# One of five gathered token chunks takes its U products from the dense pass

## The chip, the core and the metric

The program runs on one core of one Trainium2 chip. The metric is the time of one execution on the device in microseconds. TensorE is PE, VectorE is DVE, ScalarE is ACT, GpSimd is POOL, SyncE is SP. TensorE's full clock is 2.4 GHz; a granted clock of 0.50 is 1.2 GHz.

## The reference

One decoder layer on 1024 tokens of 1024 channels: a token mixer with a layer norm, then a PEER expert network with a layer norm. The change touches the expert network alone. For each token it scores 2 x 128 keys for each of 8 heads, picks the best 16 of the key pairs of each head (128 experts of 16,384), and computes

```
act = gelu(x . u_tab[idx])            # 128 dot products of length 1024 per token
out = sum over e of (g[e] * act[e]) * v_tab[idx[e]]
```

where g is the softmax over a head's 16 sums. `u_tab` and `v_tab` are 16,384 x 1024 in float32, 64 MB each.

## The kernel before

The tokens are eight chunks of 128. Chunks 0 to 4 are computed **sparse**: for each of the 128 experts of a chunk, GpSimd gathers one row per token (128 rows of 4 KB, 0.52 MB) into a ring of five slots (`gather_rows`), and DVE either reduces it against the tokens (`L143`, rows of U, into `hid`) or adds it with its factor (`L149`, rows of V, into `acc`). A chunk has 256 such steps, first 128 of U, then 128 of V; steps are numbered from 0 to `NROW` - 1 = 1279 over all five chunks and are called **rows** here. Chunk c has rows 256c to 256c + 255. A gather waits until the row five places back is used. Rows 0 to 448 lie beside earlier stages (projection, attention, merge, scores); `R_SCORE` is 449.

Chunks 5 to 7 are computed **dense** in `ffn`. The U pass (`table_block`) goes over all 16,384 experts in 128 blocks: a block of U is loaded into a ring of four (issued from ACT), PE makes 8 matmuls of 384 columns (3 chunks of 128 tokens), ACT applies gelu (`L1794`) and stores the result to `h` in DRAM. In three windows of 16 blocks (from blocks 30, 58 and 86), the weight matrix of one dense chunk is made from one-hot tiles: DVE makes them (`onehots`, `L1831`), ACT scales them (`gated`, `L1765` and `L1766`), PE multiplies them (`weight_group`, `L1697` and `L1698`, 32 groups a window), ACT copies them out, and the SP queue stores 8 MB. The V pass goes over the 128 blocks again: for each four blocks DVE multiplies the reloaded weights and h (`product`, `L1839`), and PE makes 6 matmuls a block with V (`L1716`).

**What sets the order.** Every engine runs its own list in the order of the code. DVE's list is a list of rows: `dense_row(u)` names the row that goes with block u, one-hots, products and the pieces of `choose` (136 steps that pick the experts of one chunk) stand ahead of fixed rows, so DVE's progress in rows and PE's progress in blocks bind each other at the one-hots and at the products. Before, 2.3 rows go with each block of either pass: the U pass is rows 455 to 749, the V pass rows 749 to 1044, the last product (31) stands ahead of row 1037, and 236 rows come after the V pass. `CHOICE_SPAN` places the choices of chunks 5, 6, 7, 3 and 4. After the last row DVE makes the layer norm of chunk 4 and of the three dense chunks.

Of the kernel before, what the change touches and what calls it, by code (L numbers as in the profile page):

```python
# [7 lines left out]
ALU = mybir.AluOpType  # L8
ACT = mybir.ActivationFunctionType
# [6 lines left out]
P = 128  # L16
D = 1024
# [24 lines left out]
NR = 5  # L42
NROW = 2 * NSEL * NSP
NT = 136
# [60 lines left out]


def gather_rows(nc, pool, M, A, a, b):

    ring = M["ring"]
    for n in range(a, min(b, NROW)):  # L110
        c, r = divmod(n, 2 * NSEL)
# [17 lines left out]
def use_rows(nc, dve, M, a, b):  # L129

    ring, hid, gg, acc, used = M["ring"], M["hid"], M["gg"], M["acc"], M["used"]
    for n in range(a, b):
        c, r = divmod(n, 2 * NSEL)
        e = r % NSEL
        x1 = M["x1"](c)
        if r == NSEL:
            dve.wait_ge(M["hid_gelu"], c + 1)
            nc.vector.tensor_tensor(hid[:, c % 2, :], hid[:, c % 2, :], gg[:, c, :], ALU.mult)
            dve.drain()
# [1185 lines left out]
def choose(nc, dve, M, S, sco, c, o, k0, k1):  # L1325
# [9 lines left out]
    for k in range(k0, k1):  # L1335
# [97 lines left out]
        elif k == 133:  # L1433
            ka, kb = keys_of[:, 0, :], keys_of[:, 1, :]
            if c < NSP:
                nc.vector.scalar_tensor_tensor(idx[:, c, :], ka, float(NKEY), kb, ALU.mult, ALU.add)
            else:
                if c - NSP >= 2:
                    dve.wait_ge(S["tri_mm"], c - NSP - 1)
                nc.vector.tensor_copy(pick[:, (c - NSP) % 2, 0:2, :], keys_of)  # L1440
# [96 lines left out]
for _j in range(NBLK // 4):  # L1537
    PRODUCT_AT.setdefault(min(dense_row(NBLK - 2 + 4 * _j), NROW - 1), []).append(_j)
GELU_BLOCK = {2: int((2 * 2 * NSEL + NSEL - R_SCORE - 6) / ROWS_A_BLOCK)}
EXP_BLOCK = {5: 21, 6: 48, 7: 76, 3: 108}  # L1540


def ffn(nc, ctx, M, A, out):
# [102 lines left out]
    @block.gpsimd  # L1646
    def _(pool):
        def finished(c, k):
            pool.wait_ge(sparse_done, k)
            pool.dma_start(out[P * c:P * c + P, :], x1(c)).then_inc(sparse_stored, 16)  # L1650

        for n in range(R_MERGE + NR, NROW):
            gather_rows(nc, pool, M, A, n, n + 1)
            if n == 600:
                finished(0, 1)
                finished(1, 2)
            if n == 3 * 2 * NSEL + 40:
                finished(2, 3)
            if n == 4 * 2 * NSEL + 40:
                finished(3, 4)  # L1660
        finished(4, 5)

    @block.tensor
    def _(pe):
        turn_row(pe, M, XROWS[0], 0, turned)
        for i in range(NX):
# [3 lines left out]
            score_row(pe, M, i, s_out, s_mm, True)  # L1670
        pe.wait_ge(x1t_done, ND)
        pe.wait_ge(s_out, 4 * NX)

        def table_block(u):
# [46 lines left out]
    def _(act):  # L1721
        def high(i):
            act.wait_ge(turned, i + 1)
            if i >= 2:
                act.wait_ge(s_mm, 4 * (i - 2) + 4)
            d = XROWS[i] - NSP
            if d >= 0:
                act.activation(x1t[:, :, P * d:P * d + P],
# [48 lines left out]
        for u in range(NBLK):  # L1777
# [14 lines left out]
            if u % 4 == 0 and g4 >= 2:  # L1792
                act.wait_ge(h_st[g4 % 2], 16 * (g4 // 2))
            act.activation(hout[g4 % 2][:, u % 4, :], ps[:, 4 + u % 4, 0:DT], ACT.Gelu).then_inc(h_out, 1)  # L1794
            if u + 4 < NBLK:
                act.dma_start(ut[u % 4], A["u_t"][u + 4]).then_inc(u_in[u % 4], 16)
            if u % 4 == 3:
                act.wait_ge(h_out, u + 1)
                act.dma_start(A["h"][g4], hout[g4 % 2]).then_inc(h_st[g4 % 2], 16)
# [6 lines left out]
        gate_exps(act, M, S, CHOICES.index(4))  # L1806
        for c in (3, 4):
            gate_hidden(act, M, c)

    @block.vector  # L1810
    def _(dve):
# [34 lines left out]
        for i in range(NX):  # L1846
            low(i)
            if i == 2:
                dve.wait_ge(iota_in, 16)
            if i >= 2:  # L1850
                pick_chunk(2, 34 * (i - 2), 34 * (i - 2) + 34)
            use_rows(nc, dve, M, *SCORE_ROWS[i])
        for n in range(R_SCORE, NROW):
# [172 lines left out]
def build_mix(nc, ctx, A, out):  # L2026
# [61 lines left out]
    with ExitStack() as late:  # L2088
# [100 lines left out]
```

## Time and profile before

| | us |
|---|---|
| median of 3 runs | 3952.82 (3951.11 to 3956.78) |
| profiled execution, its own time | 3949.0 |
| its span, first to last instruction | 3947.2 |
| busy PE / DVE / ACT / POOL | 2912.5 / 2829.9 / 810.7 / 1646.3 |

The profile is one execution. A share of busy time over the whole span mixes stages with different limits, so the rows of the last section are cut by stage. A POOL instruction is the making of one gather's descriptors, not its transfer. PE's matmul durations overlap each other; the spacing of what follows them is the safer measure.

### The profile page before, as it was taken

To read this page: it belongs to the slowest core of one execution; us is meant where nothing else is said; L and a number is where in the kernel's file an instruction comes from. 1 tells how busy PE (TensorE), PEld (TensorE's weight loads), DVE (VectorE), ACT (ScalarE), POOL (GpSimd) and SP (SyncE) were. 2 spreads that over 40 slices of the span, in tenths; PEclk is the share of its full clock that TensorE was granted. 3 is DMA by queue.
4 is the path that set the end of the run, shared out by engine and by line. 5 is a ranking of instruction groups with operands and counts; after the bars stand their busy time and mean duration, and the time that the engine had idled before them with its cause. 6 is when DMAs were issued, how large, how long until landed. Compare 5 with 4: busy or idle time off the path is not lost.

```text
span 3947.2 us, 40352 instructions
## 1 busy us (share of the span) xinstructions
PE 2912.5 (74%) x14133; PEld 1731.2 (44%) x14161; DVE 2829.9 (72%) x5410; ACT 810.7 (21%) x1885; POOL 1646.3 (42%) x1321
## 2 busy tenths in 40 slices
PE   7479819965999986763996889899798999960000
PEld 5458406553666553421453545465343444420000
DVE  5646485966777566966878969794777666677777
ACT  6334101112222221100110829281000000000000
POOL 5200002233444334744344333342544545667774
PEclk9779959987999898986998999899899999985555
DMA  9369224445878558977698898999999999999996
GB/s 293 117 244 391 91 79 161 154 150 184 268 259 265 186 200 333 369 251 289 218 369 305 266 371 301 382 315 375 359 385 383 390 408 408 407 332 321 315 321 216
DMA packets 309467, 1127.62 MB, mean 286 GB/s; under 512 B 33425, under 2 KB 43281, under 8 KB 305937
## 3 DMA queue, kind: packets, MB, share of 16 engines
q0 software_dynamic: 185040, 673.79, 47.6%
q1 hardware_dynamic: 101184, 358.97, 24.2%
q10 hardware_dynamic: 23040, 92.28, 6.4%
q8 instruction: 113, 1.85, 0.2%
q14 instruction: 90, 0.73, 0.1%
HBM read 996.46 MB, written 128.45 MB: 285 GB/s over the span
## 4 chain that ended last, share of the span: by engine, by line
DMA 22%; DVE 16%; POOL 8%; PE 3%; issue 3%; DVEq 1%; ACT 0%; ACTq 0%
DMA rows<-v,expert_ids 14%; DMA rows<-u,expert_ids 8%; POOL rows L117 8%; DVE rows L143 4%; DVE row_sums L149 4%; DVE branches L1831 3%; PE ps L102 1%; PE ps L104 1%; PE ps L103 1%; PE ps L1679 1%; DVE scores_in L1424 0%; DVE shared_64k L1839 0%; DVE best_key_ids L1355 0%; DVE key_sums L1429 0%; DVE scores_in L1347 0%
## 5 line engine op out<-in xcount | busy, mean ns | idle before, releaser
L117 POOL DMA_INDIRECT rows<-u,expert_ids x640 | 796.2, 1244 | 1335.1 <-DVE hidden_sums L143 821.2
L117 POOL DMA_INDIRECT rows<-v,expert_ids x640 | 770.4, 1204 | 796.9 <-DVE row_sums L149 649.9
L149 DVE SCALAR_TENSOR_TENSOR row_sums<-rows,hidden_sums,row_sums 128x1024 f32<-128x1024 f32 x630 | 796.8, 1282 | 319.3 <-DMA rows<-v,expert_ids 316.3
L1679 PE MATMUL ps<-turned_rows,mixer_state 128*128 128x384 f32 x2048 | 686.1, 495 | 23.0 <-DMA mixer_state<-u_t 22.2
L1716 PE MATMUL ps<-shared_64k 128*128 128x512 f32 x1536 | 669.6, 598 | 43.4 <-DVE shared_64k L1839 43.4
L143 DVE CUSTOM_DVE_ANT_0 rows<-rows,branches 128x1024 f32<-128x1024 f32 x384 | 468.4, 1222 | 174.4 <-DMA rows<-u,expert_ids 169.5
L1679 PEld LDWEIGHTS ps<-turned_rows,mixer_state 128*128 128x128 f32 x2048 | 391.9, 194 | 288.8 <-DMA mixer_state<-u_t 24.1
L1716 PEld LDWEIGHTS ps<-shared_64k 128*128 128x128 f32 x1536 | 294.1, 192 | 418.7 <-issue 418.6
L102 PE MATMUL ps<-x_hi_t_b,shared_64k 128*128 128x384 f16 x912 | 300.6, 330 | 89.5 <-DMA shared_64k<-w_pairs_kept 88.6
L143 DVE CUSTOM_DVE_ANT_0 rows<-rows,x_first 128x1024 f32<-128x1024 f32 x256 | 305.2, 1224 | 43.4 <-DMA rows<-u,expert_ids 40.8
L103 PE MATMUL ps<-x_lo_t_b,shared_64k 128*128 128x384 f16 x912 | 300.3, 329 | 0.0
L104 PE MATMUL ps<-x_hi_t_b,shared_64k 128*128 128x384 f16 x912 | 299.9, 329 | 0.0
L1765 ACT ACTIVATE branches<-branches,picks_t 128x128 f16<-128x128 f16 x384 | 151.2, 394 | 77.2 <-DVE branches L1831 76.7
L126 ACT ACTIVATE hidden_sums<-hidden_sums 128x128 f32<-128x128 f32 x5 | 1.5, 309 | 801.6 <-DVE hidden_sums L143 801.6
L102 PEld LDWEIGHTS ps<-x_hi_t_b,shared_64k 128*128 128x128 f16 x912 | 90.5, 99 | 148.7 <-DMA shared_64k<-w_pairs_kept 89.1
L1766 ACT ACTIVATE branches<-branches,picks_t 128x128 f16<-128x128 f16 x384 | 150.6, 392 | 0.0
L1794 ACT ACTIVATE branches<-ps 128x384 f32<-128x384 f32 x128 | 62.3, 487 | 384.8 <-PE ps L1679 384.7
L1831 DVE TENSOR_TENSOR branches<-picks_t,iota_sb 128x512 f16<-128x512 f32 x192 | 123.0, 683 | 0.8
L104 PEld LDWEIGHTS ps<-x_hi_t_b,shared_64k 128*128 128x128 f16 x912 | 90.1, 99 | 60.6 <-issue 2.7
L103 PEld LDWEIGHTS ps<-x_lo_t_b,shared_64k 128*128 128x128 f16 x912 | 90.1, 99 | 56.3 <-issue 2.4
L460 DVE SCALAR_TENSOR_TENSOR shared_64k<-conv_in_b,dw_sb_b,shared_64k 128x768 f32<-128x768 f32 x120 | 113.1, 1027 | 0.0
L1697 PE MATMUL ps<-branches 128*128 128x128 f16 x384 | 53.8, 227 | 76.7 <-ACT branches L1766 76.7
(530 smaller groups left out, 4609.6 us busy)
## 6 DMA issues: line engine op xcount, KB each, us to landing
mixer_state<-u_t ACTq DMA_DIRECT2D x128, 512.0 KB, 7.4
shared_64k<-v SPq DMA_DIRECT2D x128, 512.0 KB, 7.7
rows<-strips SPq DMA_DIRECT2D x32, 768.0 KB, 6.7
h_kept<-branches ACTq DMA_DIRECT2D x32, 768.0 KB, 9.9
shared_64k<-weights_kept SPq DMA_DIRECT2D x32, 768.0 KB, 10.9
shared_64k<-h_kept SPq DMA_DIRECT2D x32, 768.0 KB, 14.6
shared_64k<-s_pairs_kept SPq DMA_DIRECT2D x32, 512.0 KB, 6.7
rows<-w_t SPq DMA_DIRECT2D x30, 512.0 KB, 5.6
```

The costliest lines, as they stand in the source:

```text
L102: pe.matmul(out, a_hi, b_hi, start=first, stop=False)
L103: pe.matmul(out, a_hi, b_lo, start=False, stop=False)
L104: return pe.matmul(out, a_lo, b_hi, start=False, stop=last)
L117: nc.gpsimd.indirect_dma_start(ring[:, n % NR, :], None, A["u" if r < NSEL else "v"], bass.IndirectOffsetOnAxis(ap=M["idx"][:, c, e:e + 1] ...
L143: nc.vector.tensor_tensor_reduce(src, src, x1, 1.0, 0.0, ALU.mult, ALU.add, hid[:, c % 2, e:e + 1]).then_inc(used, 1)
L149: nc.vector.scalar_tensor_tensor(acc[:, e % 2, :], src, hid[:, c % 2, e:e + 1], acc[:, e % 2, :], ALU.mult, ALU.add).then_inc(used, 1)
L460: nc.vector.scalar_tensor_tensor(acc, src, w, acc, ALU.mult, ALU.add).then_inc(tap, 1)
L1679: m = pe.matmul(ps[:, 4 + u % 4, 0:DT], uk[u % 4][:, k, :], x1t[:, k, :], start=k == 0, stop=k == KD - 1)
L1716: m = pe.matmul(ps[:, 2 + 2 * d + half, :], pr[j // 4 % 3][:, d, j % 4, :], vt[j % 6][:, 512 * half:512 * half + 512], start=j == 0, stop= ...
L1765: act.activation(ah[:, n % 4, t, :], o1[:, n % 4, t, :], ACT.Copy, scale=pt[:, 3, tok])
L1766: ins = act.activation(o1[:, n % 4, t, :], o1[:, n % 4, t, :], ACT.Copy, scale=pt[:, 2, tok])
L1831: ins = nc.vector.tensor_tensor(to[:, n % 4, :, :], pt[:, f, 4 * q:4 * q + 4].rearrange("p (t o) -> p t o", o=1).to_broadcast([P, 4, NKEY] ...
```

## The change

Chunk 4 (`HYB`) becomes a hybrid. Its tokens are a fourth group of 128 columns in the U pass: each of the 8 matmuls of a block has 512 columns (`UT`) for 384. ACT makes a second gelu from columns 384 to 511 into a small tile and, for each pair of blocks, stores it to a new DRAM array `h_side` (16,384 x 128 tokens, 8.4 MB, runs of 512 bytes). The 128 gathers of U rows for chunk 4 are gone, `NROW` is 1152. In their place GpSimd makes 128 gathers of one number per token from `h_side` straight into `hid` (`gather_values`), one ahead of each row gather from row 878 (`VALUES_FROM`) on. DVE waits for all of them at row 1024, where the V rows of chunk 4 begin.

The pace is changed too: 2.9 rows go with a block of the U pass and 2.1 with a block of the V pass. The U pass is rows 453 to 824, the V pass rows 824 to 1093, the last product stands ahead of row 1080, and 59 rows come after the V pass. The choices of chunks 5, 6, 7, 3 are spread over rows 453 to 511, 522 to 589, 603 to 670 and 690 to 757, that of chunk 4 over rows 777 to 870 (before: 451 to 497, 509 to 561, 573 to 627, 637 to 701, 737 to 837). The gelu of chunk 2 moves on ACT from block 80 to block 64.

```diff
+HYB = NSP - 1
+UT = DT + P
-NROW = 2 * NSEL * NSP
+NROW = 2 * NSEL * NSP - NSEL
+def row_at(n):
+    c = min(n // (2 * NSEL), HYB)
+    return c, n - 2 * NSEL * c + NSEL * (c == HYB)
...
         if r == NSEL:
-            dve.wait_ge(M["hid_gelu"], c + 1)
+            if c == HYB:
+                dve.wait_ge(M["values_in"], 16 * NSEL)
+            else:
+                dve.wait_ge(M["hid_gelu"], c + 1)
...
-            if c < NSP:
+            if c == HYB:
+                nc.vector.scalar_tensor_tensor(posf[:, 0, :], ka, float(NKEY), kb, ALU.mult, ALU.add)
+                dve.drain()
+                nc.vector.tensor_copy(idx[:, c, :], posf[:, 0, :])
+                nc.vector.tensor_scalar(M["place"], posf[:, 0, :], float(P), M["lane"], ALU.mult, ALU.add)
+            elif c < NSP:
...
-ROWS_A_BLOCK = 2.3
-CHOICE_SPAN = {5: (2, 48), 6: (60, 112), 7: (124, 178), 3: (188, 252), 4: (288, 388)}
+ROWS_U_BLOCK = 2.9
+ROWS_V_BLOCK = 2.1
+CHOICE_SPAN = {5: (0, 20), 6: (24, 47), 7: (52, 75), 3: (82, 105), 4: (112, 150)}
-    return int(R_SCORE + 6 + ROWS_A_BLOCK * u)
+    return int(R_SCORE + 4 + ROWS_U_BLOCK * min(u, NBLK) + ROWS_V_BLOCK * max(u - NBLK, 0))
...
+VALUES_FROM = dense_row(CHOICE_SPAN[HYB][1]) + NR + 3
...
+        def gather_values(e):
+            if e == 0:
+                pool.wait_ge(M["chosen"], HYB + 1)
+                for i in range(2):
+                    pool.wait_ge(side_st[i], 16 * (NBLK // 4))
+            if e < NSEL:
+                nc.gpsimd.indirect_dma_start(
+                    M["hid"][:, HYB % 2, e:e + 1], None, A["h_side"],
+                    bass.IndirectOffsetOnAxis(ap=M["place"][:, e:e + 1], axis=0)).then_inc(M["values_in"], 16)
         for n in range(R_MERGE + NR, NROW):
+            if n >= VALUES_FROM:
+                gather_values(n - VALUES_FROM)
             gather_rows(nc, pool, M, A, n, n + 1)
...
-                m = pe.matmul(ps[:, 4 + u % 4, 0:DT], uk[u % 4][:, k, :], x1t[:, k, :], start=k == 0, stop=k == KD - 1)
+                m = pe.matmul(ps[:, 4 + u % 4, 0:UT], uk[u % 4][:, k, :], x1t[:, k, :], start=k == 0, stop=k == KD - 1)
...
-            act.activation(hout[g4 % 2][:, u % 4, :], ps[:, 4 + u % 4, 0:DT], ACT.Gelu).then_inc(h_out, 1)
+            act.activation(hout[g4 % 2][:, u % 4, :], ps[:, 4 + u % 4, 0:DT], ACT.Gelu)
+            if u % 2 == 0 and u >= 4:
+                act.wait_ge(side_st[u // 2 % 2], 16 * (u // 4))
+            act.activation(side[:, u // 2 % 2, u % 2, :], ps[:, 4 + u % 4, DT:UT], ACT.Gelu).then_inc(h_out, 1)
...
+            if u % 2:
+                act.wait_ge(h_out, u + 1)
+                act.dma_start(A["h_side_blocks"][u // 2], side[:, u // 2 % 2]).then_inc(side_st[u // 2 % 2], 16)
```

## Rows read from the trace of the kernel before

**Rows 1.** The page, the span in 40 equal slices, busy tenths.
```profile
PE   7479819965999986763996889899798999960000
PEclk9779959987999898986998999899899999985555
```

**Rows 2.** Busy time by stage: us, PE, PEld, DVE, ACT, POOL; PEclk, DMA.
```profile
1978.00:2184.00 206.00, 164.50 (x524) 97.18 (x524) 174.73 (x444) 32.16 (x75) 92.38 (x84) 0.89 0.90 335
2184.00:2378.00 194.00, 165.89 (x690) 101.31 (x688) 162.26 (x433) 105.34 (x314) 65.08 (x63) 0.92 0.90 324
2378.00:2563.00 185.00, 166.06 (x709) 101.40 (x708) 158.64 (x407) 108.16 (x326) 68.76 (x66) 0.94 0.93 348
2563.00:2667.00 104.00, 102.26 (x510) 63.99 (x509) 97.69 (x227) 90.86 (x281) 41.07 (x38) 1.00 0.90 314
2667.00:2806.00 139.00, 130.39 (x399) 76.14 (x397) 71.24 (x90) 14.76 (x28) 42.92 (x40) 0.98 0.98 378
2806.00:2829.00 23.00, 0.00 (x1) 0.00 (x0) 18.53 (x24) 1.77 (x2) 14.40 (x13) 0.55 0.97 353
2829.00:3518.00 689.00, 668.61 (x1534) 293.95 (x1535) 482.20 (x742) 1.90 (x3) 378.98 (x301) 0.98 1.00 387
3518.00:3698.00 180.00, 1.04 (x3) 0.19 (x1) 130.78 (x213) 0.00 (x0) 131.29 (x108) 0.51 0.92 323
3701.00:3913.00 212.00, 0.00 (x0) 0.00 (x0) 163.65 (x131) 0.00 (x0) 156.56 (x125) 0.50 0.89 312
3913.00:3947.00 34.00, 0.00 (x0) 0.00 (x0) 27.16 (x64) 0.00 (x0) 0.57 (x1) 0.50 0.15 62
```

**Rows 3.** Timeline of ACT: start, us, instruction, [idle before <-releaser].
```profile
1998.73 0.49 ACT L1794 ACTIVATE branches<-ps 128x384 f32<-128x384 f32 x1 [4.67 <-PE ps L1679]
2003.89 0.49 ACT L1794 ACTIVATE branches<-ps 128x384 f32<-128x384 f32 x1 [4.67 <-PE ps L1679]
...
2400.84 0.49 ACT L1794 ACTIVATE branches<-ps 128x384 f32<-128x384 f32 x1
...
2432.35 0.49 ACT L1794 ACTIVATE branches<-ps 128x384 f32<-128x384 f32 x1
```

**Rows 4.** Timeline of PE, the first weight product of windows 0 and 1.
```profile
2172.93 0.29 PE L1697 MATMUL ps<-branches 128*128 128x128 f16 x1 [39.74 <-ACT branches L1766]
...
2371.86 0.29 PE L1697 MATMUL ps<-branches 128*128 128x128 f16 x1 [9.81 <-ACT branches L1766]
```

**Rows 5.** Groups in 2829:3518: busy us, mean ns | idle before <-releasers.
```profile
L1716 PE MATMUL ps<-shared_64k 128*128 128x512 f32 x1534 | 668.8, 598 | 43.4 <-DVE shared_64k L1839 43.4
...
L117 POOL DMA_INDIRECT rows<-v,expert_ids x148 | 194.9, 1317 | 139.9 <-DVE row_sums L149 115.1 <-issue 16.6 <-DVE hidden_sums L143 6.6
L149 DVE SCALAR_TENSOR_TENSOR row_sums<-rows,hidden_sums,row_sums 128x1024 f32<-128x1024 f32 x150 | 191.9, 1283 | 113.4 <-DMA rows<-v,expert_ids 113.2
```

**Rows 6.** Timeline of POOL and DVE in 3345:3375.
```profile
3343.72 1.75 DVE L1839 TENSOR_TENSOR shared_64k<-shared_64k 128x1536 f32<-128x1536 f32 x1
3344.07 2.21 POOL L117 DMA_INDIRECT rows<-v,expert_ids  x1 [1.73 <-DVE row_sums L149]
...
3353.52 1.28 DVE L149 SCALAR_TENSOR_TENSOR row_sums<-rows,hidden_sums,row_sums 128x1024 f32<-128x1024 f32 x1 [0.87 <-DMA rows<-v,expert_ids]
...
3353.77 1.85 POOL L117 DMA_INDIRECT rows<-v,expert_ids  x1 [0.30 <-issue]
...
3360.06 0.94 POOL L117 DMA_INDIRECT rows<-v,expert_ids  x1 [0.30 <-issue]
```

**Rows 7.** DMA totals of 1978:2806 and of 2829:3518.
```profile
DMA packets 67801, 281.48 MB, mean 340 GB/s; under 512 B 7438, under 2 KB 7438, under 8 KB 66472
...
DMA packets 76417, 266.64 MB, mean 387 GB/s; under 512 B 7663, under 2 KB 7663, under 8 KB 76394
```

**Rows 8.** Timeline of DVE: the last product, and the end of chunk 4.
```profile
3494.61 1.75 DVE L1839 TENSOR_TENSOR shared_64k<-shared_64k 128x1536 f32<-128x1536 f32 x1
...
3911.68 1.23 DVE L153 TENSOR_TENSOR row_sums<-row_sums 128x1024 f32<-128x1024 f32 x1
```

More of the change, by code:

```diff
@@ L110, in gather_rows @@
     for n in range(a, min(b, NROW)):
-        c, r = divmod(n, 2 * NSEL)
+        c, r = row_at(n)
         e = r % NSEL
@@ L132, in use_rows @@
     for n in range(a, b):
-        c, r = divmod(n, 2 * NSEL)
+        c, r = row_at(n)
         e = r % NSEL
@@ L1517, with block_at @@
 WINDOW_AT = [30, 58, 86]
-ROWS_A_BLOCK = 2.3
-CHOICE_SPAN = {5: (2, 48), 6: (60, 112), 7: (124, 178), 3: (188, 252), 4: (288, 388)}
+ROWS_U_BLOCK = 2.9
+ROWS_V_BLOCK = 2.1
+CHOICE_SPAN = {5: (0, 20), 6: (24, 47), 7: (52, 75), 3: (82, 105), 4: (112, 150)}
 NORM_AT = {520: 0, 528: 1}
 def dense_row(u):
-    return int(R_SCORE + 6 + ROWS_A_BLOCK * u)
+    return int(R_SCORE + 4 + ROWS_U_BLOCK * min(u, NBLK) + ROWS_V_BLOCK * max(u - NBLK, 0))
+def block_at(row):
+    return next(u for u in range(2 * NBLK) if dense_row(u) >= row)
 CHOICE_AT = {}
-for _c, (_a, _b) in CHOICE_SPAN.items():
+for _c, (_u, _v) in CHOICE_SPAN.items():
+    _a, _b = dense_row(_u), dense_row(_v)
     for _n in range(_a, _b):
-        CHOICE_AT.setdefault(R_SCORE + _n, []).append((_c, NT * (_n - _a) // (_b - _a), NT * (_n - _a + 1) // (_b - _a)))
+        CHOICE_AT.setdefault(_n, []).append((_c, NT * (_n - _a) // (_b - _a), NT * (_n - _a + 1) // (_b - _a)))
 ONEHOT_AT = {}
@@ L1538 @@
     PRODUCT_AT.setdefault(min(dense_row(NBLK - 2 + 4 * _j), NROW - 1), []).append(_j)
-GELU_BLOCK = {2: int((2 * 2 * NSEL + NSEL - R_SCORE - 6) / ROWS_A_BLOCK)}
-EXP_BLOCK = {5: 21, 6: 48, 7: 76, 3: 108}
+GELU_BLOCK = {2: block_at(5 * NSEL) - 1}
+EXP_BLOCK = {5: 21, 6: 48, 7: 76, 3: 106}
+VALUES_FROM = dense_row(CHOICE_SPAN[HYB][1]) + NR + 3
 def ffn(nc, ctx, M, A, out):
@@ L1557, in ffn @@
     again = ut
+    side = M["side"]
     iota, pick, pt, gh16 = M["iota"], M["pick"], M["pick_t"], M["gh16"]
@@ L1568, in ffn @@
     h_st = [sem(f"h_stored{i}") for i in range(2)]
+    side_st = [sem(f"side_stored{i}") for i in range(2)]
+    lane_in = sem("lane_in")
     tri_mm, tri_hi, tri_out, tri_lo = (sem(n) for n in "tri_mm tri_hi tri_out tri_lo".split())
@@ L1585, in _ @@
         sp.dma_start(iota[:], A["iota"]).then_inc(iota_in, 16)
+        sp.dma_start(M["lane"], A["iota"][0:1, :].rearrange("o n -> n o")).then_inc(lane_in, 16)
         for d in range(ND):
@@ L1670, in _ @@
             score_row(pe, M, i, s_out, s_mm, True)
-        pe.wait_ge(x1t_done, ND)
+        pe.wait_ge(x1t_done, ND + 1)
         pe.wait_ge(s_out, 4 * NX)
@@ L1725, in high @@
                 act.wait_ge(s_mm, 4 * (i - 2) + 4)
-            d = XROWS[i] - NSP
-            if d >= 0:
+            d = XROWS[i] - NSP if XROWS[i] >= NSP else ND
+            if XROWS[i] >= HYB:
                 act.activation(x1t[:, :, P * d:P * d + P],
@@ L1793, in _ @@
                 act.wait_ge(h_st[g4 % 2], 16 * (g4 // 2))
-            act.activation(hout[g4 % 2][:, u % 4, :], ps[:, 4 + u % 4, 0:DT], ACT.Gelu).then_inc(h_out, 1)
+            act.activation(hout[g4 % 2][:, u % 4, :], ps[:, 4 + u % 4, 0:DT], ACT.Gelu)
+            if u % 2 == 0 and u >= 4:
+                act.wait_ge(side_st[u // 2 % 2], 16 * (u // 4))
+            act.activation(side[:, u // 2 % 2, u % 2, :], ps[:, 4 + u % 4, DT:UT], ACT.Gelu).then_inc(h_out, 1)
             if u + 4 < NBLK:
                 act.dma_start(ut[u % 4], A["u_t"][u + 4]).then_inc(u_in[u % 4], 16)
+            if u % 2:
+                act.wait_ge(h_out, u + 1)
+                act.dma_start(A["h_side_blocks"][u // 2], side[:, u // 2 % 2]).then_inc(side_st[u // 2 % 2], 16)
             if u % 4 == 3:
-                act.wait_ge(h_out, u + 1)
                 act.dma_start(A["h"][g4], hout[g4 % 2]).then_inc(h_st[g4 % 2], 16)
@@ L1806, in _ @@
         gate_exps(act, M, S, CHOICES.index(4))
-        for c in (3, 4):
-            gate_hidden(act, M, c)
+        gate_hidden(act, M, 3)
     @block.vector
@@ L1849, in _ @@
                 dve.wait_ge(iota_in, 16)
+                dve.wait_ge(lane_in, 16)
             if i >= 2:
@@ L1862, in _ @@
                 second_norm(NORM_AT[n])
-            if n >= 2 * 2 * NSEL and n % (2 * NSEL) == 2 * NSEL - 1:
-                second_norm(n // (2 * NSEL))
+            if n >= 2 * 2 * NSEL and row_at(n)[1] == 2 * NSEL - 1:
+                second_norm(row_at(n)[0])
         for d in range(ND):
@@ L2043, in build_mix @@
     M["stage_sems"] = {}
+    M["values_in"] = sem("values_in")
     M["mp_in"] = [sem(f"folded_in{i}") for i in range(4)]
@@ L2063, in build_mix @@
     for n, shape, dt in (("weights", (ND, P, NBLK * P), F32), ("h", (NBLK // 4, P, 4, DT), F32),
+                         ("h_side", (NEXP * P, 1), F32),
                          ("scores", (T // P, P, 2 * H * NKEY), F32), ("x1", (ND, P, D), F32),
@@ L2067, in build_mix @@
         A[n] = nc.dram_tensor(n + "_kept", shape, dt, kind="Internal").ap()
+    A["h_side_blocks"] = A["h_side"].rearrange("(b j e t) o -> b e j (t o)", j=2, e=P, t=P)
     A["v_blocks"] = A["v"].rearrange("(b e) c -> b e c", e=P)
@@ L2097, in build_mix @@
             nc.release_semaphore(handle)
-        M["x1t"] = sb("turned_rows", [P, KD, DT], F32)[:]
+        M["x1t"] = sb("turned_rows", [P, KD, UT], F32)[:]
+        M["place"], M["lane"] = sb("value_places", [P, NSEL], U32)[:], sb("lane_sb", [P, 1], F32)[:]
+        M["side"] = mixa[:, 4 * D:4 * D + 4 * P].rearrange("p (s j t) -> p s j t", s=2, j=2)
         M["sco"] = [sb("scores_in", [P, 2 * H * NKEY], F32)[:]]
```

## The prediction

> **What bounds the kernel now.** The first view is the page's 40 slices: PE is nearly full up to about 3520 us and does nothing after it, at a clock of 0.5 [rows 1]. The second is the busy time by stage [rows 2], where the program splits into four parts.
>
> The U pass runs from 1978 to 2806 (828 us). The timeline of ACT gives PE's pace there: outside the windows one gelu each 5.16 us, with ACT idle before it until PE is done [rows 3]. That is PE's own time: a block is 8 matmuls of 384 columns. Inside window 1 five blocks take 31.51 us, 6.30 each [rows 3]; the extra 1.14 us a block is the weight products. So PE's own time for the pass is 128 x 5.16 + 48 x 1.14 = 715 us, and the other 113 us are stalls. The largest is PE's wait of 39.7 us at the first weight product, a second is 9.8 us [rows 4]: ACT had no one-hots, since DVE had not reached their row. In the stages that hold the windows DVE is busy 0.84 to 0.94 of the time; behind them the DMA share is up to 0.98 [rows 2]. The pass is thus bound by PE, and in places by DVE and the rows that it waits for.
>
> From 2806 to 2829 PE stands still: DVE is late at the row of product 0 [rows 2].
>
> The V pass takes 689 us (2829 to 3518), PE is busy 668.8 of them [rows 5], so 660 = 128 x 5.16 us is its floor (6 x 512 columns are as many as 8 x 384). DMA is at a share of 1.00 and 387 GB/s, DVE waits 113.4 us for rows of V [rows 2, 5]: PE and DMA are both full.
>
> Then come the rows that have no partner: 212 us for 126 rows, 1.68 us each [rows 2]. From the last product at 3494.6 to the end of chunk 4 at 3911.7 there are 417 us and 243 rows [rows 8], and 35.5 us of norms and store up to 3947.2. The end of the kernel is therefore V pass, then leftover rows, then a fixed tail.
>
> **What the change removes.** 128 rows of U (67 MB) go, and the new pace packs more of the rest beside the dense passes: behind the last product stand 1152 - 1080 = 72 rows instead of 243. At 1.68 us that is 121 us, for the 417 of before.
>
> **What it adds to the U pass.** 512 columns for 384: 5.16 x 4/3 = 6.88 us a block, + 1.72 us, 220 us in all. Nothing hides it where PE is the limit; it hides where PE waited. PE's floor becomes 128 x 6.88 + 48 x 1.14 = 935 us. The stalls must be worked out anew.
>
> At the entry, PE reaches block 30 at 1978 + 30 x 6.88 = 2184. DVE reached row 521 and its one-hots shortly before 2173 [rows 4]; now it has to be at row 537, 16 rows x 1.3 us = 21 us further, but the choice of chunk 6 stands mostly behind that row now (about 10 us less). It comes to about 2184, and slower loads of U leave DMA room for rows. I take 5 us of stall for the 40.
>
> For a window, DVE's stage 2563:2667 shows 97.7 of 104 us busy [rows 2], so DVE was full. It gets 0.6 rows x 1.28 us = 0.8 us more a block, 6.4 to 7.2, where PE goes from 6.30 to 8.02. So PE, not DVE, is the limit inside a window. Between windows 12 blocks now take 83 us. Their transfers are 12 x 0.52 MB of U, 12 x 0.20 of h, 12 x 0.07 of `h_side`, 35 rows x 0.52, 8.4 MB of weights and 1 MB of scores, 37 MB; at the V pass's 387 GB/s [rows 7] 96 us. Some of that spills into the windows, where DMA has room. I take 10 us of stall for each of the two gaps, 10 behind window 2 for the same store, 0 at best and 25 each at worst. Sum: 935 + 5 + 30 = 970 us, + 142 on before. Over the whole pass DMA isn't the limit: 281 MB of before [rows 7], 40 MB of rows and 8.4 MB more are 330 MB, 340 GB/s, below the 387 of the V pass. DVE gets 77 rows x 1.28 = 99 us and about half a choice (22 us) more, in 142 us.
>
> The second gelu on ACT (128 columns, about 0.3 us), the wait for its store and one more DMA issue each two blocks add some 0.6 us a block; ACT idles 4.67 us a block outside the windows [rows 3] and is busy 90.86 of 104 in one [rows 2], 5.6 us of a block that grows to 8.0. They cost nothing. What is queued behind ACT's wait for the side store is that block's gelu and the next window's `gated`; the store has two blocks' time, 13.8 us. The gelu of chunk 2 now stands inside window 1 and can hold ACT until row 640; DVE is at row 638 there, so 0 to 5 us, in the stall above. Product 0 stands ahead of row 818, and DVE is no longer late by a store: 4 us for the 23.
>
> **What it adds to the V pass.** A value gather is new; no row shows one. On POOL, a row gather that meets no DVE instruction takes 0.94 us, with 0.30 behind it. One that starts under a DVE instruction ends 0.82 us after that instruction: 3353.77 + 1.85 = 3355.62, where `L149` ended at 3354.80; 3344.07 + 2.21 = 3346.28 against `L1839`'s 3345.47 [rows 6]. The mean of the pass is 1.32 us for rows of V [rows 5]. A value gather also makes one descriptor for each of 128 tokens, so I price it like a row gather: 1.24 us at least, 1.62 at the mean. Row n's gather stands behind value gather n - 878, so POOL spends 2.5 to 3.2 us a row, while PE's pace asks for 5.16 / 2.1 = 2.46. With both engines free about half of the time I take 1.5 us each, 3.0 a row: POOL is the limit for 128 rows, DVE falls behind, the products with it, and PE waits. Cost (3.0 - 2.46) x 128 = 69 us, taken as 65; from 5 to 95.
>
> The Trainium skill (SBUF — State Buffer, "Who interferes with whom") says that an operation with two SBUF inputs takes only the read side of the port that VectorE shares with GpSimd, and infers that making descriptors needs the write side, so that such an operation shouldn't hold a gather up. By it each gather would take 1.24 us, the pair 2.48, and this term would be near nothing. The rows show otherwise [rows 6]: `L1839` and `L149` both have two SBUF inputs and both held a gather.
>
> Transfers: 2.1 rows and one block of V, weights and h are 2.02 MB per 5.16 us, 391 GB/s, what the pass has now (387). The 4-byte packets of the value gathers are not in any row as reads; between nothing and a row packet's time they cost 0 to 163 us (128 x 8 packets an engine x 0.159 us, that being 4096 B at the 412 GB/s / 16 of a full stage). In the 65 us by which POOL stretches the stage there is room for the small end, and I take the small end, as packets under 512 B already are a tenth of all packets [rows 7] beside a full DMA. The Trainium skill (DMA: Bandwidth & Descriptors, "Measured") gives some 10.5 ns as the least for a packet; by that estimate it would be 11 us of DMA time.
>
> Early in the pass PE lost 20 us (43.4 less the 23 at its start [rows 5]) to DVE, busy with chunk 4's choice; half of that choice is done before now: 15 us. V pass: 660 + 15 + 65 = 740 us.
>
> **Sum.** 1978 + 970 + 4 + 740 = 3692 for the end of the V pass. The last product starts 24 us before it, as now (3518 - 3494.6): 3668. Then 1.75 of product [rows 8], 121 of rows, 35.5 of tail: a span of 3826. The profiled execution took 3949.0 for a span of 3947.2, so 3828, or 121 less; off the median 3952.8 that is 3832 us.
>
> **The rivals.** (1) *The value gathers ride free*: POOL's slack, 139.9 us before 148 rows of V [rows 5], 0.95 a row, nearly covers one of 1.24. Against it, the gathers held under DVE. 3832 - 65 = 3767. (2) *The U pass keeps its stalls*: DVE and DMA bind at the windows as now, 113 us instead of 35, since more rows go with each block. For it, DMA shares of 0.90 to 0.98 [rows 2]; against, 33% more PE time a block under only 26% more rows. 3832 + 78 = 3910. (3) *A value gather is much dearer than a row gather*, on POOL in rows 878 to 1005: each microsecond costs 128 us there. It decides from 121 / 128 = 0.95 us above my 1.5, 2.45 us each; at 3 us the kernel takes 3832 + 192 = 4024, slower than before. For it, one gather of 2.21 us [rows 6]; against, that this was a wait for a DVE operation. (4) *Nothing is removed*, which the new `NROW` excludes.
>
> **Chances.** The forecast 0.5, (1) 0.2, (2) 0.2, (3) 0.1, of which 0.07 beyond its point. The range of 3758 to 3902 takes in (1) with a few us less of stalls, and most of (2); what is left out is the far side of (2) and (3). A change of 0.2% (8 us) is about what can be told from none. Faster 0.91, within it 0.02, slower 0.07.
>
> **What would show it.** Gelus of `L1794` 6.88 us apart outside windows; no 40 us wait at the first weight product; a U pass near 970 us. In rows 878 to 1005 POOL without idle time, row steps of 3.0 us, PE waiting for `L1839`; before and behind that, 2.46. After the last product 72 rows at 1.68. The forecast falls if the U pass is over 1010 us, or if PE never waits in the V pass, or if DVE waits at row 1024 for values.

## The result and the profile after

The changed kernel took 3827.66 us (median of 4 runs, 3819.65 to 3836.34) beside 3951.97 before: a ratio of 0.9685, 95% interval 0.9659 to 0.9711. 3832 us was forecast. The profiled execution took 3836.3 us, its span is 3834.5.

| part of the span, us | before | forecast | after |
|---|---|---|---|
| start of the U pass | 1978 | 1978 | 1985 |
| U pass | 828 | 970 | 983 |
| gap before the V pass | 23 | 4 | 2 |
| V pass | 690 | 740 | 739 |
| last product to the end of chunk 4's last row | 417 | 123 | 122 |
| tail | 35.5 | 35.5 | 35.5 |
| span | 3947 | 3826 | 3834.5 |

The last product starts before the V pass ends (24 us before, 32 us after), so the rows add up to more than the span.

The page's slices, for [rows 1]: PE is full to nearly the end, and the stretch at clock 0.5 is gone.

```profile
PE   6579828965999995873799899899999998699960
PEclk9779969977999997996899999999999999799985
```

The stages, for [rows 2], same columns (us, PE, PEld, DVE, ACT, POOL, clock, DMA share, GB/s). The first five are the U pass. The next five are the V pass without its last 31 us, which lie in the eleventh, beside the rows behind the last product. Rows 878 to 1005, those with a value gather ahead of each, are 3115 to 3498.

```profile
1985.00:2214.00 229.00, 211.25 (x503) 94.27 (x504) 193.83 (x472) 34.19 (x95) 104.38 (x99) 0.96 0.93 343
2214.00:2440.00 226.00, 213.08 (x710) 101.08 (x709) 180.44 (x466) 114.28 (x354) 89.19 (x84) 0.97 0.92 333
2440.00:2660.00 220.00, 212.10 (x712) 100.62 (x711) 179.85 (x381) 114.75 (x355) 89.66 (x82) 0.98 0.92 338
2660.00:2785.00 125.00, 125.00 (x500) 61.92 (x499) 113.95 (x271) 93.81 (x294) 54.38 (x48) 1.00 0.91 316
2785.00:2969.00 184.00, 176.94 (x408) 77.75 (x406) 121.03 (x258) 20.02 (x55) 80.36 (x68) 0.98 0.97 372
2969.00:3115.00 146.00, 136.93 (x315) 60.46 (x316) 113.81 (x272) 2.88 (x3) 80.45 (x61) 0.98 0.97 371
3115.00:3242.00 127.00, 121.35 (x277) 52.66 (x276) 66.21 (x72) 0.31 (x1) 100.10 (x89) 0.99 0.93 334
3242.00:3318.00 76.00, 36.20 (x39) 10.59 (x38) 32.59 (x25) 0.00 (x0) 56.32 (x54) 0.54 0.72 230
3318.00:3498.00 180.00, 179.90 (x417) 79.57 (x417) 87.69 (x67) 0.00 (x0) 128.76 (x112) 0.99 0.94 347
3498.00:3678.00 180.00, 180.00 (x421) 79.65 (x420) 117.55 (x103) 0.00 (x0) 95.34 (x77) 1.00 1.01 396
3678.00:3799.00 121.00, 30.59 (x72) 13.26 (x70) 92.01 (x73) 0.00 (x0) 80.56 (x68) 0.64 0.89 321
3800.00:3834.00 34.00, 0.00 (x0) 0.00 (x0) 27.42 (x65) 0.00 (x0) 0.57 (x1) 0.50 0.15 62
```

In the U pass PE is busy 0.92 to 1.00 of each stage. POOL rises to 0.71 to 0.79 busy in the value rows; DMA falls there from 371 GB/s to 334 and 347, and rises to 396 behind them. The stretch 3242:3318 is another matter: PE busy 36 of 76 us at a clock of 0.54. It comes back below.

The gelus of ACT are 6.87 us apart outside windows, 5.16 before [rows 3]:

```profile
2102.40 0.49 ACT L1834 ACTIVATE branches<-ps 128x384 f32<-128x384 f32 x1 [6.21 <-PE ps L1719]
...
2109.27 0.49 ACT L1834 ACTIVATE branches<-ps 128x384 f32<-128x384 f32 x1 [6.21 <-PE ps L1719]
```

PE in that stretch (timeline of the changed kernel). Ahead of each matmul stand up to 1.8 us for which the profile has no releaser; the longest such wait is 3.2 us:

```profile
3257.06 1.87 PE L1756 MATMUL ps<-shared_64k 128*128 128x512 f32 x2 [1.79 <-issue]
3259.89 1.01 PE L1756 MATMUL ps<-shared_64k 128*128 128x512 f32 x1 [0.97 <-issue]
...
3267.67 0.59 PE L1756 MATMUL ps<-shared_64k 128*128 128x512 f32 x1 [1.41 <-issue]
3269.77 1.01 PE L1756 MATMUL ps<-shared_64k 128*128 128x512 f32 x1 [1.51 <-issue]
```

### The profile page after: what moved, and what is told of

Same layout as the page of the kernel before. It is cut to its first block, busy times and chain, and to the rows that moved or that the text cites. A ratio compares the mean times of both kernels' runs of the same rounds, so it can differ in the third digit from the quotient of the medians.

```text
span 3834.5 us, 40292 instructions
## 1 busy us (share of the span) xinstructions
PE 3138.2 (82%) x14133; PEld 1729.4 (45%) x14161; DVE 2667.6 (70%) x5156; ACT 835.9 (22%) x2013; POOL 1613.7 (42%) x1321
## 4 chain that ended last, share of the span: by engine, by line
PE 17%; DMA 14%; POOL 7%; DVE 6%; issue 4%; another core or an unknown queue 3%; ACT 1%; DVEq 0%; SPq 0%; ACTq 0%
PE ps L1719 13%; DMA rows<-v,expert_ids 7%; POOL rows L125 5%; DMA rows<-u,expert_ids 5%; POOL hidden_sums L1686 2%; DVE rows L154 2%; DMA h_side_kept<-mixer_state 1%; DVE row_sums L160 1%; PE ps L104 1%; PE ps L106 1%; PE ps L105 1%; DMA mixer_state<-u_t 1%; PE ps L1737 1%; PE ps L1738 1%
## 5 line engine op out<-in xcount | busy, mean ns | idle before, releaser
L125 POOL DMA_INDIRECT rows<-u,expert_ids x512 | 648.4, 1266 | 1214.0 <-DVE hidden_sums L154 697.1
L125 POOL DMA_INDIRECT rows<-v,expert_ids x640 | 744.8, 1164 | 798.9 <-DVE row_sums L160 632.4
L160 DVE SCALAR_TENSOR_TENSOR row_sums<-rows,hidden_sums,row_sums 128x1024 f32<-128x1024 f32 x630 | 796.0, 1282 | 354.7 <-DMA rows<-v,expert_ids 323.3
L1719 PE MATMUL ps<-turned_rows,mixer_state 128*128 128x512 f32 x2048 | 899.1, 598 | 11.4 <-DMA mixer_state<-u_t 10.7
L1756 PE MATMUL ps<-shared_64k 128*128 128x512 f32 x1536 | 685.0, 605 | 55.7 <-issue 42.9
L154 DVE CUSTOM_DVE_ANT_0 rows<-rows,branches 128x1024 f32<-128x1024 f32 x256 | 310.8, 1219 | 109.3 <-DMA rows<-u,expert_ids 100.6
L1805 ACT ACTIVATE branches<-branches,picks_t 128x128 f16<-128x128 f16 x384 | 153.2, 399 | 43.0 <-DVE branches L1875 42.9
L1686 POOL DMA_INDIRECT hidden_sums<-h_side_kept,value_places x128 | 141.3, 1104 | 39.0 <-issue 39.0
L104 PE MATMUL ps<-branches,shared_64k 128*128 128x384 f16 x192 | 65.6, 342 | 54.8 <-DMA shared_64k<-s_pairs_kept 54.7
```

The source lines that it names most:

```text
L104: pe.matmul(out, a_hi, b_hi, start=first, stop=False)
L125: nc.gpsimd.indirect_dma_start(ring[:, n % NR, :], None, A["u" if r < NSEL else "v"], bass.IndirectOffsetOnAxis(ap=M["idx"][:, c, e:e + 1] ...
L154: nc.vector.tensor_tensor_reduce(src, src, x1, 1.0, 0.0, ALU.mult, ALU.add, hid[:, c % 2, e:e + 1]).then_inc(used, 1)
L160: nc.vector.scalar_tensor_tensor(acc[:, e % 2, :], src, hid[:, c % 2, e:e + 1], acc[:, e % 2, :], ALU.mult, ALU.add).then_inc(used, 1)
L1686: nc.gpsimd.indirect_dma_start(M["hid"][:, HYB % 2, e:e + 1], None, A["h_side"], bass.IndirectOffsetOnAxis(ap=M["place"][:, e:e + 1], axis ...
L1719: m = pe.matmul(ps[:, 4 + u % 4, 0:UT], uk[u % 4][:, k, :], x1t[:, k, :], start=k == 0, stop=k == KD - 1)
```

## Experiments

**The changed kernel again**, twice, nothing edited.

> The changed kernel once more, nothing edited. The first profile has a stretch of some 75 us in the V pass (3242 to 3318) in which PE, DVE and SP all go slowly and the trace names no releaser. If it comes again at the same block, it belongs to the program; if not, to that execution. Expected 3828 us (3815 to 3840) either way, since rows 878 to 1005 still cost POOL 2.8 us each: the stall is then found as PE waits for products, spread over the pass.

> The changed kernel a third time, beside the next two. In three of the four kernels with value gathers ahead of every row one stretch of 50 to 95 us in those rows was slow on all engines with no releaser in the trace; in one (the same program as here) it did not come. If it comes, the time is near 3825 us and the stretch lies in rows 878 to 1005; if not, near 3805.

Measured 3805.6 us, ratio 0.9633 (0.9604 to 0.9662), and 3806.61, ratio 0.9642 (0.9615 to 0.9669). The slow stretch is in neither profile, and both are 21 us faster than the first result. The first expectation, 3815 to 3840 us with or without the stretch, is missed; the second holds. (It counts four kernels with a value gather ahead of every row and leaves out the one with 3.2 rows a block, which had no such stretch either.) The U pass takes 983 us and 978, the V pass 718 and 713. Without the stretch, PE waits for products over the whole of the value rows (groups in the V pass, of the first of the two):

```profile
L1756 PE MATMUL ps<-shared_64k 128*128 128x512 f32 x1536 | 678.2, 604 | 41.0 <-DVE shared_64k L1883 41.0
```

So part of the first result's V pass was that stretch. Comparisons below are with these two repeats.

**The value gathers.**

```diff
-                dve.wait_ge(M["values_in"], 16 * NSEL)
+                pass
...
-            if n >= VALUES_FROM:
-                gather_values(n - VALUES_FROM)
```

> The 128 value gathers and DVE's wait for them are left out (the factors of chunk 4 are then stale numbers); all else stays. Theory, POOL's issue rate sets the pace of rows 878 to 1005 (2.84 us a row against 2.46): the V pass shortens by 45 to 75 us, 3755 to 3783 us in all. Rival, PE and DMA bind the pass anyway: within 15 us of the changed kernel, 3813 to 3828.

Measured 3744.62 us, ratio 0.9475 (0.9451 to 0.9499), 61 us below the kernel beside it; the total expected was reckoned from the first result and is missed, the 45 to 75 us are met. PE's V pass takes 662 us where it took 718: 56 us. POOL's groups in 3107:3475, first with the value gathers, then without:

```profile
L1686 POOL DMA_INDIRECT hidden_sums<-h_side_kept,value_places x124 | 144.3, 1164 | 37.8 <-issue 37.8
L125 POOL DMA_INDIRECT rows<-v,expert_ids x115 | 130.5, 1135 | 36.0 <-issue 34.8 <-DVE row_sums L160 1.2
```

```profile
L125 POOL DMA_INDIRECT rows<-v,expert_ids x144 | 180.2, 1251 | 159.1 <-DVE row_sums L160 129.5 <-issue 13.5 <-DVE row_sums L157 11.0
```

With them POOL has nothing but the 0.30 us behind each instruction as idle time: 37.8 us for 124. It is full, at 1.16 + 0.30 us for a value gather and 1.14 + 0.30 for a row: 2.9 us a row (DVE is at row 880 at 3107.8 us and at row 1000 at 3458.4: 2.92), where PE's pace is 2.46. Without them it waits for used rows. The DMA totals of 3107:3475, with and without:

```profile
DMA packets 39714, 123.74 MB, mean 336 GB/s; under 512 B 7473, under 2 KB 7473, under 8 KB 39704
```

```profile
DMA packets 42454, 147.38 MB, mean 400 GB/s; under 512 B 4198, under 2 KB 4198, under 8 KB 42443
```

With value gathers DMA moves less (336 against 400 GB/s) and has 3275 packets under 512 B more. The trace has their sizes. Every gather, of a row or of values, ends in 16 packets of 4 bytes, and a value gather has 16 packets of 32 bytes beside them (1985 such packets in this stretch for 124 value gathers, none without them), not 128 of 4 bytes. They take 14 ns each. DMA is not what binds there.

**The same gathers, spread.**

```diff
-CHOICE_SPAN = {5: (0, 20), 6: (24, 47), 7: (52, 75), 3: (82, 105), 4: (112, 150)}
+CHOICE_SPAN = {5: (0, 20), 6: (24, 47), 7: (52, 75), 3: (82, 105), 4: (110, 128)}
...
-                gather_values(n - VALUES_FROM)
+                k = n - VALUES_FROM
+                for e in range(2 * k // 3, 2 * (k + 1) // 3):
+                    gather_values(e)
```

> The same 128 value gathers, but two for every three rows over rows 832 to 1023 instead of one a row over 878 to 1005; chunk 4's choice over blocks 110 to 128 so that the places are known in time. Theory, POOL's issue rate is what makes the value gathers cost 56 us in the V pass: three row gathers and two value gathers take 3 x 1.5 + 2 x 1.4 = 7.3 us against 3 x 2.46 = 7.4 of PE's pace, so nearly all of it goes, 3755 to 3785 us. Rival, the packets and the landing of the values cost DMA time: the same number of them costs the same wherever they stand, 3795 to 3815. Second rival: the denser choice costs in the U pass what is won.

Measured 3783.95 us, ratio 0.9557 (0.9533 to 0.9581). The V pass takes 688 us for 718. The number of gathers and of their bytes is the same, so the 30 us go with where they stand on POOL. This run was made on another chip (10) than the repeats (14); the spread kernel further down, on chip 14, has a V pass of 669 us beside a repeat's 713. Of the rest, 12.6 us are one wait of PE for product 1. The expectation of the kernel with the earlier choice, below, lays it to exponentials that ACT makes after the U pass. The trace says otherwise: ACT has them 21 us before DVE uses them, and DVE has no idle time before that. It works without a pause on the last, large steps of the choice, which stand between products 0 and 1:

```profile
2973.41 0.31 ACT L1474 ACTIVATE exponents<-exponents 128x128 f32<-128x128 f32 x1
...
2987.56 2.77 DVE L1435 TENSOR_TENSOR scores_in<-scores_in,key_sums 128x256 f32<-128x256 f32 x8
2990.41 2.29 DVE L1440 TENSOR_REDUCE key_sums<-scores_in 128x128 f32<-128x2048 f32 x1
...
2994.70 0.27 DVE L1458 TENSOR_REDUCE gate_sum<-exponents 128x8 f32<-128x128 f32 x1
```

**Columns alone**, in the kernel before.

```diff
-                m = pe.matmul(ps[:, 4 + u % 4, 0:DT], uk[u % 4][:, k, :], x1t[:, k, :], start=k == 0, stop=k == KD - 1)
+                m = pe.matmul(ps[:, 4 + u % 4, 0:UT], uk[u % 4][:, k, :], x1t[:, k, :], start=k == 0, stop=k == KD - 1)
```

> The kernel before with 512 columns instead of 384 in the matmuls of the U pass, the extra columns used by nobody; rows, pace and gathers as before. Theory, PE's own time binds the U pass and the stalls of DVE shrink as it slows: the pass goes from 828 to 940 to 975 us, 3952 + 110 to 145 = 4062 to 4097 in all. Rival, DVE and DMA bind the pass enough to hide half of the added PE time: under 4030. Second rival, the stalls stay whole: 4172.

Measured 4023.09 us, ratio 1.0177 (1.0149 to 1.0206): 71 us more, below the 110 that my theory gave at least, and within the first rival's bound. Of 220 us of added PE time, 120 were hidden in the U pass and the gap behind it (from the start of one pass to that of the other it is 851 us before, 136 over PE's floor of 715, and 950 here, 15 over the floor of 935), and 25 more in the V pass (690 before, 665 here), since DVE now enters it on time. The sum 220 - 120 - 25 = 75 is near the 71 measured. The pass itself, at 950, lies where I had put it; what I had left out was that the old gap of 23 us and the V pass's stalls go with the U pass's. PE's wait at the weight products, 76.7 us before, of which 39.7 at once [rows 4], is now (waits in the U pass: total, times, longest):

```profile
PE ps L1699 <- ACT branches L1768: 13.6, 5, 10.2
```

**Rows in the U pass, more and fewer.** More: 3.2 a block.

```diff
-ROWS_U_BLOCK = 2.9
-CHOICE_SPAN = {5: (0, 20), 6: (24, 47), 7: (52, 75), 3: (82, 105), 4: (112, 150)}
-EXP_BLOCK = {5: 21, 6: 48, 7: 76, 3: 106}
+ROWS_U_BLOCK = 3.2
+CHOICE_SPAN = {5: (0, 20), 6: (24, 47), 7: (52, 75), 3: (80, 96), 4: (110, 140)}
+EXP_BLOCK = {5: 21, 6: 48, 7: 76, 3: 95}
```

> The changed kernel with 3.2 rows a block in the U pass instead of 2.9; chunk 3's choice over blocks 80 to 96 and chunk 4's over 110 to 140, so that they are in time. 38 rows move from behind the last product into the U pass. Theory, PE binds the U pass and has room for them: 38 x 1.68 = 64 us less behind the V pass, 10 to 40 more in the U pass, 3775 to 3805 us. Rival, the rows of the U pass are at the limit of DVE and DMA: each added row costs there what it saves behind, 3825 us or more.

Measured 3802.2 us, ratio 0.9614 (0.9586 to 0.9643): no change against 3805.6, the intervals overlapping. The time lies in the theory's range only because that was reckoned from 3828; as a difference it is the rival's, no gain. Behind the last product 57 us went (120 to 63), but the U pass and its gap took 1047 us for 983. The two passes, first with 3.2 rows, then with 2.9:

```profile
1974.00:3020.00 1046.00, 947.23 (x2825) 438.45 (x2824) 841.46 (x1968) 378.63 (x1149) 484.12 (x417) 0.95 0.92 340
3020.00:3747.00 727.00, 680.65 (x1536) 297.18 (x1536) 443.18 (x474) 1.90 (x3) 491.66 (x413) 0.97 0.96 358
```

```profile
1977.00:2960.00 983.00, 935.46 (x2825) 434.12 (x2825) 789.17 (x1844) 375.72 (x1148) 436.89 (x379) 0.98 0.93 342
2960.00:3679.00 719.00, 678.22 (x1536) 296.64 (x1536) 445.09 (x558) 3.25 (x5) 486.40 (x412) 0.97 0.96 361
```

DVE gains 52 us of work and the pass 63. But 29 of the 63 lie in blocks 94 to 102, which take 90 us for 61, and into these the edit had pressed chunk 3's choice. So the run doesn't show that the added rows alone cost what they save; 3.2 rows with a choice spread as before were not run.

Fewer: 2.3 in both passes.

```diff
-ROWS_U_BLOCK = 2.9
-ROWS_V_BLOCK = 2.1
+ROWS_U_BLOCK = 2.3
+ROWS_V_BLOCK = 2.3
```

> The changed kernel with 2.3 rows a block in both passes, as before the change; the choices keep their blocks. The last product stands ahead of row 1034, so 118 rows come behind it instead of 72, 77 us more at 1.66. Theory, the U pass then comes near its floor (950 us for 983), and the V pass is bound by POOL in the value rows as now: 3840 to 3870 us. Rival, the pace is worth nothing, since each row costs the same in the U pass as behind the V pass: 3795 to 3815.

Measured 3908.44 us, ratio 0.9865 (0.9837 to 0.9893), above the range expected. The U pass with its gap is 945 us (38 less), the rows behind the last product take 210 (90 more, 77 foreseen: the last product stands ahead of row 1028, not 1034, so 52 rows are added and not 46). The V pass takes 766 instead of 718. I had left out that at 2.3 rows a block PE's pace is 2.24 us a row against POOL's 2.9, (2.46 - 2.24) x 128 = 28 us by estimate; but PE waits for products 0.7 us in this whole V pass, so that price is not seen. What is seen are waits of PE without a releaser (V pass: total, times, longest), most of them in two stretches, blocks 43 to 51 and 64 to 70:

```profile
PE ps L1756 <- issue: 59.0, 74, 2.1
```

These blocks take 95 and 68 us, where 5.16 a block would make 66 of both: 98 us, nearly all that the pass has over the 662 without value gathers. So the total is no measure of what the pace is worth. Outside the V pass the old pace wins 38 us and loses 90.

**The side results.** The second gelu and the stores are left out, the value gathers read numbers from the table of U.

```diff
-            act.activation(side[:, u // 2 % 2, u % 2, :], ps[:, 4 + u % 4, DT:UT], ACT.Gelu).then_inc(h_out, 1)
...
-                act.dma_start(A["h_side_blocks"][u // 2], side[:, u // 2 % 2]).then_inc(side_st[u // 2 % 2], 16)
...
-                    M["hid"][:, HYB % 2, e:e + 1], None, A["h_side"],
+                    M["hid"][:, HYB % 2, e:e + 1], None, A["u_flat"],
```

> The second gelu and the 64 stores of side results are left out, and the value gathers read from the table of U instead (the same number of 4-byte reads; chunk 4's factors are then no hidden values). Theory, ACT and DMA have room for both in the U pass: within 8 us of the changed kernel, 3797 to 3813. Rival, the 8.4 MB in runs of 512 bytes or ACT's waits for them cost at the windows: 15 to 40 us less.

Measured 3825.69 us, ratio 0.9666 (0.9645 to 0.9688), outside both ranges and not faster. Its profile has the slow stretch (waits of PE in the V pass), in blocks 68 to 73, and a V pass of 753 us, so the total can't settle the question. Its U pass with gap takes 972 us for 984 and 985 in the repeats, which ran on another chip: side results cost about 12 us there at most.

```profile
PE ps L1754 <- issue: 30.4, 37, 3.3
```

**Two steps on.** The values spread, chunk 4's choice over blocks 106 to 124 with its exponentials in ACT's list of the U pass; and then all exponentials earlier. The first against the changed kernel (the spread is as above), then the second against the first:

```diff
-CHOICE_SPAN = {5: (0, 20), 6: (24, 47), 7: (52, 75), 3: (82, 105), 4: (112, 150)}
+CHOICE_SPAN = {5: (0, 20), 6: (24, 47), 7: (52, 75), 3: (82, 105), 4: (106, 124)}
...
-EXP_BLOCK = {5: 21, 6: 48, 7: 76, 3: 106}
-VALUES_FROM = dense_row(CHOICE_SPAN[HYB][1]) + NR + 3
+EXP_BLOCK = {5: 21, 6: 48, 7: 76, 3: 106, 4: 124}
+VALUES_FROM = dense_row(NBLK) + NR + 3
```

```diff
-EXP_BLOCK = {5: 21, 6: 48, 7: 76, 3: 106, 4: 124}
+EXP_BLOCK = {5: 19, 6: 46, 7: 74, 3: 104, 4: 123}
```

> Two value gathers for three rows over rows 832 to 1023, chunk 4's choice over blocks 106 to 124 with its exponentials at block 124, so that DVE need not wait for ACT's end of the U pass at the start of the V pass. Theory: the wait of 12.6 us of PE for product 1 goes, 3765 to 3785 us. Rival, the choice costs the same elsewhere: no change on spreading alone, 3780 to 3795.

> The same, with the exponentials of the choices of chunks 5, 6, 7, 3 two blocks earlier in ACT's list (19, 46, 74, 104), and that of chunk 4 one. Theory: what is left of the stalls at the windows (17.9, 11.4 and 8.2 us of PE) comes largely from DVE's waits for these exponentials (51.8 us in five, 20.4 and 15.8 the longest), during which it falls behind: 15 to 35 us less than the kernel beside it, 3740 to 3765. Rival, DVE would wait for gathered rows instead, DMA being at 0.93 to 0.96 there: within 8 us of the kernel beside it.

Measured 3771.02 us, ratio 0.9564 (0.9531 to 0.9597), and 3754.33 us, ratio 0.9523 (0.9495 to 0.9551), beside 3806.61 for the changed kernel. The V pass of the first takes 669 us, 7 more than without value gathers. But PE now waits 15.8 us for product 0 ahead of it: the same last steps of chunk 4's choice, which DVE does without waiting for exponentials, now stand ahead of product 0. The wait has moved, not gone, and by its ratio this kernel is no faster than the spread alone (0.9557). The time lies in the theory's range; its reason is wrong, and the rival's stands.

In the second a cause of the stalls at the windows is seen. DVE stood still for an exponential (a repeat of the changed kernel, [idle before <-releaser]), was behind by the time the window came, and PE waited there. Waits in the U pass of that repeat:

```profile
2359.78 0.29 DVE L1458 TENSOR_REDUCE gate_sum<-exponents 128x8 f32<-128x128 f32 x1 [20.35 <-ACT exponents L1474]
```

```profile
DVE gate_sum L1458 <- ACT exponents L1474: 51.8, 5, 20.4
...
PE ps L1737 <- ACT branches L1806: 43.4, 8, 17.9
```

and with the exponentials earlier, where one long wait of 8.3 us is left and the U pass takes 962 us, for 978 in the kernel with the spread alone beside it:

```profile
PE ps L1739 <- ACT branches L1808: 17.7, 8, 6.7
...
DVE gate_sum L1458 <- ACT exponents L1474: 9.8, 2, 8.3
```

PE's waits at the first weight products of the three windows go from 15.1, 9.9 and 6.3 us to 6.7 and none over 3. The total is 17 us less, with intervals that just overlap. Such a wait costs only where DVE has no slack behind it: with 2.3 rows a block (the columns-alone kernel) DVE waits 94.1 us for exponentials, and PE 13.6 at the weight products.

The V pass of the second: PE waits 14.2 us in all, 9.7 of it for product 0.

```profile
L1758 PE MATMUL ps<-shared_64k 128*128 128x512 f32 x1536 | 663.1, 594 | 14.2 <-DVE shared_64k L1884 14.2
```

## Why the prediction was right

It was right in the total and in most terms. The closeness of the total, 4 us, is partly luck: the repeats, without the stretch, are 26 us below the forecast.

**U pass.** 935 us of floor held: 6.87 us between gelus, 950 us with the columns alone. I had 35 us of stalls and 4 of gap; there were 48 and 2 (48 and 43 us of stalls in the repeats). The places were named (entry, gaps, behind window 2), the entry mis-sized: 5 us foreseen, 15.6 to 17.9 measured at the first weight product. The reason given for the gaps, DMA bytes, was not the main one: PE waited 3.4 and 4.3 us for blocks of U in the repeats (10.7 in the first result), while DVE waited 51.8 us for exponentials that stand late in ACT's list, and setting these two blocks earlier took 16 us out of the pass. The prediction had no term for such waits.

**V pass.** That POOL would bind in the value rows was right and shown twice: without the gathers PE waits 4.2 us in the whole pass (662 us), and the same gathers spread cost 26 us of it. 65 us was forecast, 56 measured; the price of 1.5 us for each instruction was 1.44 and 1.46. It was a choice between 1.24 and 1.62 with "about half of the time" as its ground, so the closeness is some luck too. My 15 us for the early part were about 2: half of chunk 4's choice was done before. 713 to 718 us is what the value rows alone give, for 740 forecast; the first result's 739 holds a stretch that nothing in the forecast covers, and the two errors met.

**Behind the V pass.** 72 rows at 1.68 us: forecast 123 us with the product, measured 122. The first result's U pass began 7 us later than forecast, and its last product 8 us earlier before the end of the V pass; these two cancel.

**Rivals.** That value gathers ride free falls with the 56 us. That the U pass keeps its stalls falls with the 48. (Its own figure, 3910, lies outside the range of 3758 to 3902 that was said to take in most of it.) That a value gather is much dearer falls with 1.16 us. Packets: I had counted one for each token, at up to 0.159 us, up to 163 us of DMA time. There are 16 of data for each value gather, at 14 ns each, some 2 us by estimate if the 16 DMA engines share them, and DMA was emptier than without them. (The 412 GB/s of that sum stands in no row; 408 is the most of a 100 us stretch of the V pass.)

**Gathers held by DVE.** The rows of the prediction hold for the whole V pass of the kernel before. 140 gathers issued while DVE was idle took 0.93 to 0.97 us. Of 126 issued under `L143`, `L149` or `L1839`, 124 ended 0.81 to 0.82 us after that operation did. In the value rows, where POOL never pauses, its mean is 1.14 to 1.16 us for instructions that take 0.94 alone, and a row took 2.92 us. The Trainium skill (SBUF — State Buffer, "Who interferes with whom") says that a `tensor_tensor` takes only the read side of the port that VectorE shares with GpSimd, and infers that making descriptors needs the write side; by that no gather would have been held by `L160` or `L1883`, and the pair of gathers would have taken 2.48 us a row. The measurement goes against that inference. The same section says that an operation with two SBUF inputs does contend with a GpSimd instruction that reads SBUF; the holding would agree with it if a gather counts as one, which no run here tests.

## What to carry to other kernels

Where two engines walk lists that bind each other at fixed points, price a change by each engine's own floor between two such points, and look for the small instruction of a third engine that one of them waits for: exponentials that stood two blocks late in ACT's list cost 16 us. Before blaming such an instruction, look when it was done: at the start of the V pass it was done 21 us before its use, and with it made earlier PE's wait was still there. Count instructions on the issuing engine before bytes: on POOL 128 gathers of 4 bytes cost what 128 gathers of 4 KB cost, 56 us of the V pass, and 7 once they were spread over rows that leave POOL idle and chunk 4's choice came earlier (the whole kernel still stood at 0.9564, beside 0.9475 without them, for the choice had its wait at product 0). Work that is moved from an idle tail under a full stage is a gain only as far as that stage has slack; 3.2 rows a block, as tried, gained nothing over 2.9.

## What was not expected of the hardware

Of six profiles of kernels with a value gather ahead of each row, three (the first of the changed kernel, the one without side results, the one with the old pace) have stretches of 68 to 95 us in the value rows in which PE starts a matmul only each 1.4 to 2.8 us and the trace names no releaser: 42.9, 30.4 and 59.0 us of such waits. The changed kernel is 21 us slower with it than in the two repeats, which have none; nor have the ones with 3.2 rows a block, without value gathers and the last two. The spread one has 2.6 us.

The stretch is PE's alone. In it DVE's `L160` takes 1.28 us and POOL issues a pair of gathers each 2.8 us, beside 2.9 in the repeat; SP's loads are fewer because PE frees their tiles late. PE's weight loads (PEld) start at 1.40, 2.10, 2.80 or 3.50 us from each other, multiples of 0.70, in 33 of 34 steps over 1.2 us:

```profile
3257.07 0.29 PEld L1756 LDWEIGHTS ps<-shared_64k 128*128 128x128 f32 x1 [1.81 <-issue]
3258.49 0.29 PEld L1756 LDWEIGHTS ps<-shared_64k 128*128 128x128 f32 x1 [1.13 <-issue]
3260.59 0.29 PEld L1756 LDWEIGHTS ps<-shared_64k 128*128 128x128 f32 x1 [1.81 <-issue]
...
3266.28 0.19 PEld L1756 LDWEIGHTS ps<-shared_64k 128*128 128x128 f32 x1 [0.52 <-issue]
3268.38 0.19 PEld L1756 LDWEIGHTS ps<-shared_64k 128*128 128x128 f32 x1 [1.92 <-issue]
```

The low clock doesn't explain it: a wait of 1.5 us stands ahead of the clock's fall at 3245, and in 3265.6:3269 the clock is back at 1.00 (below, the stages of the stretch) while the loads are still 2.10 us apart.

```profile
3245.00:3265.60 20.60, 13.58 (x16) 4.13 (x15) 10.57 (x8) 0.00 (x0) 16.03 (x16) 0.50 0.67 210
3265.60:3269.00 3.40, 1.25 (x2) 0.52 (x3) 1.93 (x2) 0.00 (x0) 2.79 (x3) 1.00 0.88 305
3269.00:3318.00 49.00, 20.08 (x20) 5.75 (x20) 18.80 (x15) 0.00 (x0) 35.11 (x35) 0.50 0.74 236
```

What holds PE there is open. It was only seen while POOL issued gathers without pause. There is also a plain rival that no run tests, the chip: the record has both later kernels with the stretch on chip 10 and all three such profiles without it on chip 14, and doesn't name the chip of the first result. No kernel was run on both.

A second thing: a half-empty POOL is not a free one. Idle 0.9 us a row before, it could not take 1.24 us more.
